# Eleven convolution taps moved into an attention's steps, selection rounds put between index sums, and waits for GpSimd's weight halves

## The chip, the cores and the metric

The kernel runs on one core of a Trainium2 chip. The metric is the device time of one execution in microseconds (us), lower is better. One execution was also recorded by the hardware profiler; its rows are what this document reads.

## The reference

Two transformer blocks on 512 tokens of width 1024, all in fp32. What bears on this change is the first block's mixer (windowed attention, a 31-tap depthwise convolution, memory attention) and the second block's sparse attention with its index scores and its top-128 choice:

```python
def conformer_conv(u, w_dw, b_dw, g_ln, b_ln):
    a, gate = jnp.split(u, 2, axis=-1)
    h = a * jax.nn.sigmoid(gate)
    h = lax.conv_general_dilated(h, w_dw[:, None, :], window_strides=(1,),
        padding=((CONV_WIDTH - 1, 0),), ...) + b_dw      # CONV_WIDTH = 31, 256 channels
    return jax.nn.silu(layer_norm(h, g_ln, b_ln))
...
    x = x + jnp.concatenate([y_attn, y_conv, y_mem], axis=-1) @ w_out[l]
...
    def block_fn(args):                                  # 4 blocks of 128 queries
        qb, qib, wib, start = args
        s = jnp.einsum('bqhd,bsd->bqhs', qib, ki)        # 8 index heads
        score = jnp.einsum('bqhs,bqh->bqs', jax.nn.relu(s), wib)
        score = jnp.where(causal[None], score, -jnp.inf)
        _, sel = lax.top_k(score, topk)                  # topk = 128
        ...                                              # attention over the chosen keys
```

## The kernel before, in words

Every engine has its own program, written out in order, and engines meet only at semaphores. Weights come in tiles of 128x1024 through a ring of four slots (`w_raw`). Each fp32 weight tile is split into a high half (`w_hi`, ScalarE, L1202) and a low half (`w_lo`: VectorE's `split`, L1561, in the feed-forward parts, GpSimd's `split`, L592, in two pieces of 512 columns, in the two attention mixers). A product is then three matmuls: high by high, low by high, high by low (L675 to L677). SyncE may load a ring slot again once the low half of its tile is done, and TensorE may use a tile once its low half is done.

The work runs in stages: feed-forward part, first mixer, feed-forward part, second mixer, and two more feed-forward parts with a convolution mixer between them. In a mixer, TensorE goes through the projection tiles (`TILES_A`, `TILES_B`) one by one; index m in the code counts the tile, and ScalarE and VectorE have the same loop over m for the tile one or more places behind. Inside tile m, after its third and sixth step of eight, TensorE does small things for earlier tiles (`betweenA`, `betweenB`): sums of squares of a head pair, the spread of its inverse norm (`head_spread`, L922, which needs the reciprocal of VectorE's `head_rstd`, L1786), or the scores of two index heads (`index_pair`, L1119).

After the tiles comes the attention: a loop over pairs of heads and query blocks, u = 0, 1, 2, ... In each step TensorE makes the scores of pair u (L951, mask L954), transposes the weights of pair u-2 (L972) and multiplies pair u-3 with the values (L993); VectorE takes the row maximum of pair u (`pair_max`, L1826 on), and in every second step normalises a group of two pairs (`group_norm`, L1863, on whose result the next group's values wait) and makes its low half (L1871); ScalarE takes the exponentials (L1363). What a step does besides is in `others(u)`. Scores of even pairs lie in PSUM banks 0 and 1, of odd pairs in banks 2 and 3.

The convolution of the first mixer is 62 VectorE instructions, taps t = 0 to 30 of channel half c = 0, then of c = 1 (`conv_tap`, L1928 and L1931), each adding one shifted, weighted copy of `glu` to an accumulator in bank 2 or 3; the last tap of a half writes `conv` in SBUF. `TAPS_AT` says how many taps stand at which m. All of them end before TensorE may score pair 1, whose banks they use. The mean over channels follows from `conv` by TensorE (`conv_total`, L1047, at u = 2) and VectorE (L1980, at u = 3).

In the second mixer, blocks b = 1, 2, 3 of 128 queries have (b+1)*128 scores each, summed over eight index heads (`index_sum`, L2015 and L2018, two heads after each `index_pair`). A selection round (`take_top`) takes the eight largest away: MAX8 (L2030), then MATCH_REPLACE8 (L2032). Each block takes 16 rounds, then a mask (L2035) on which the first score of that block's attention waits. `TOPS_AT` places rounds at m, and the rest goes one by one into the attention's steps u = 1, 2, ... (`topB`). A rope (`head_rope`) is three VectorE instructions on SBUF data, L1805, L1807 and L1809.

Of the kernel before, what the change touches and what calls it, by code (L numbers as in the profile page):

```python
# [23 lines left out]
TT = T // P  # L24
# [12 lines left out]
CONV_A = 31  # L37
# [47 lines left out]
def build(nc, A, out):  # L85
    ctx = ExitStack()
    with ctx:
# [72 lines left out]
        def chunk(t, k, width=T):  # L160
            return t[:, k * width:(k + 1) * width]
# [262 lines left out]
            TOPS += [(b, "tri")] + [(b, r, s) for r in range(ROUNDS) for s in ("max", "take")] + [(b, "mask")]  # L424
        top = Marks(sem("top"), TOPS)
        ROUND_LIST = [(b, r) for b in range(1, TT) for r in range(ROUNDS)]
        TOPS_AT = {9: 3, 10: 3, 11: 2, 12: 3, 13: 3, 14: 3, 15: 3, 16: 3, 17: 2}
        TOP_EARLY = sum(TOPS_AT.values())
        TAPS_AT = {2: 3, 3: 3, 4: 6, 5: 6, 6: 5, 7: 6, 8: 3, 9: 5, 10: 5, 11: 5, 12: 4, 13: 4, 14: 4, 15: 3}

        def index_slot(m, part):

# [35 lines left out]
        def after(eng, marks, key):  # L468

            eng.wait_ge(marks.sem, marks.value[key])  # L470
# [99 lines left out]
        def _(pool):  # L570
# [89 lines left out]
            pool.wait_ge(x_done, 32)  # L660
            pool.dma_start(matsB[:, :], A["mats"]).then_inc(stage_in, 16)
            for j in range(LEAD, len(TILES_B) + KC):
                split(first_job["mixB"] + j)
            after(pool, h_roped, "qB7")
            ada_steps(2)
# [3 lines left out]
        def _(pe):  # L669
# [371 lines left out]
            betweenA(len(TILES_A), 0)  # L1041

            def sumsA(u):
                if u == 2:
                    after(pe, d_conv, (CONV_A - 1, 1))
                    for c in range(2):
                        mm = pe.matmul(bank(5), ones[:, :], chunk(conv, c), start=c == 0, stop=c == 1)  # L1047
                    mm.then_inc(p_misc.at("conv_total"), 1)
                if 5 <= u < 5 + TT:
                    b = u - 5  # L1050
                    if b == 0:
                        after(pe, a_misc, "conv_sq1")
                    for c in range(2):
                        mm = pe.matmul(bank(5)[:, b:b + 1], hsA[:, c * T + b * P:c * T + (b + 1) * P], ones[:, 0:1],
                                       start=c == 0, stop=c == 1)
                    if b == TT - 1:
                        mm.then_inc(p_misc.at("conv_var"), 1)
                if u == len(PAIRS_A) + 2:
                    out_chunk("outA", 0, oA_hi, oA_lo, ("a", 1), True)
                    after(pe, d_misc, "conv_rstd")  # L1060
                    for b in range(TT):
                        mm = pe.matmul(bank(5)[:, b * P:(b + 1) * P],
                                       hrA[:, 64 + 32 + b:64 + 32 + b + 1].to_broadcast([P, P]), identity[:, :],
                                       start=True, stop=True)
                    mm.then_inc(p_misc.at("conv_spread"), 1)
                    for k in range(1, 4):
                        out_chunk("outA", k, oA_hi, oA_lo, ("a", 2 * k + 1))

            def scoreA(pair):
                kind, j, b = pair  # L1070
                if PAIRS_A.index(pair) == 1:
                    after(pe, d_conv, (CONV_A - 1, 1))
                if b == 0 and kind == "win":
                    after(pe, h_roped, f"qA{j}")
                if b == 0 and kind == "mem":
                    after(pe, h_normed, f"mk{j}")
                    after(pe, h_scaled, f"mq{j}")
                    after(pe, v_done, f"mv{j}")
                if kind == "win":
                    n, lo = (P, 0) if b == 0 else (2 * P, (b - 1) * P)  # L1080
                    pair_score(pair, lambda rows: qA[rows, j * T + b * P:j * T + (b + 1) * P],
                               lambda rows: kA[rows, lo:lo + n], ident16A[:, :], mask16A[:, 2 * P - n:2 * P])
                else:
                    pair_score(pair, lambda rows: mq[rows, j * T + b * P:j * T + (b + 1) * P],
                               lambda rows: mk[rows, j * M:(j + 1) * M], None, None)
# [110 lines left out]
        def _(act):  # L1196
# [224 lines left out]
            for m in range(2, len(TILES_A) + 1):  # L1421
                t = TILES_A[m - 1]
# [36 lines left out]

            def conv_part(u):  # L1460

                if u == 4:
                    for c in range(2):
                        after(act, d_misc, f"ctr{c}")
                        act.activation(chunk(hsA, c), chunk(conv, c), ACT.Square).then_inc(a_misc.at(f"conv_sq{c}"), 1)
                if u == 25:
                    after(act, p_misc, "conv_var")
                    act.activation(hrA[:, 32:32 + TT], bank(5)[:, 0:TT], ACT.Sqrt, bias=tiny[:, 0:1], scale=1.0 / (2 * P))\
                        .then_inc(a_misc.at("conv_std"), 1)
                if u == 26:  # L1470
                    for c in range(2):
                        after(act, d_misc, f"conv_n{c}")
                        act.activation(chunk(conv, c), chunk(conv, c), ACT.Silu, bias=col("cln_b", c))\
                            .then_inc(a_misc.at(f"conv_y{c}"), 1)
                if u == 27:
                    for c in range(2):
                        after(act, a_misc, f"conv_y{c}")
                        act.activation(oA_hi[4 + c], chunk(conv, c), ACT.Copy).then_inc(g_hi.at(f"c{c}"), 1)
# [77 lines left out]
        def _(dve):  # L1556
# [366 lines left out]
            def conv_tap(t, c):  # L1923
                src = glu[:, c * (PAD_A + T) + t:c * (PAD_A + T) + t + T]
                w = col("w_dw", c * CONV_A + t)
                if t == 0:
                    after(dve, glu_done, f"a{c}")
                    dve.tensor_scalar(bank(2 + c), src, w, col("b_dw", c), ALU.mult, ALU.add).then_inc(d_conv.at((t, c)), 1)  # L1928
                else:
                    after(dve, d_conv, (t - 1, c))  # L1930
                    dve.scalar_tensor_tensor(chunk(conv, c) if t == CONV_A - 1 else bank(2 + c), src, w, bank(2 + c),  # L1931
                                             ALU.mult, ALU.add).then_inc(d_conv.at((t, c)), 1)

            done = 0
# [39 lines left out]
                    query_inverse("A", 8 * len(QUERIES[0]), qscA, qnsA)  # L1974

            def conv_part(u):
                if u == 3:
                    after(dve, p_misc, "conv_total")
                    for c in range(2):
                        dve.scalar_tensor_tensor(chunk(conv, c), bank(5), -1.0 / (2 * P), chunk(conv, c), ALU.mult,  # L1980
                                                 ALU.add).then_inc(d_misc.at(f"ctr{c}"), 1)
# [59 lines left out]
            for m in range(2, len(TILES_B) + 1):  # L2041
# [11 lines left out]
                              chunk({"kB": kB, "qB": qB, "qi": qi}[r[:2]], int(r[2])))  # L2053
                if m == 4:
                    head_rstd("ki")
                for b, r in ROUND_LIST[done:done + TOPS_AT.get(m, 0)]:
                    take_top(b, r)
                done += TOPS_AT.get(m, 0)
                for b, h in index_step(m):
                    index_sum(b, h)  # L2060
                if n in h_normed.value and m > 3:
                    head_norm(n, straight(n))

# [169 lines left out]
```

## Time and profile before

| what | value |
|---|---|
| median of 3 runs | 2165.54 us (2160.98 to 2165.81) |
| the profiled execution's own time | 2165.37 us |
| its span, first to last instruction | 2163.4 us |
| TensorE busy | 2135.3 us, 99% |
| VectorE busy | 1211.7 us, 56% |
| ScalarE busy | 783.2 us, 36% |
| GpSimd busy | 233.8 us, 11% |
| granted TensorE clock, mean | 0.994 |

TensorE is busy nearly all the time, so the kernel gets shorter only where TensorE waits, or where it runs at its lower clock. In the profile PE is TensorE, DVE VectorE, ACT ScalarE, POOL GpSimd.

### The profile page before, as it was taken

What the parts mean: (1) busy time and instruction counts of PE and PEld (TensorE: products, weight loads), DVE (VectorE), ACT (ScalarE), POOL (GpSimd) and SP (SyncE); (2) the same over time, 40 slices, a digit from 0 to 9 for tenths busy, and PEclk for the clock granted to TensorE, in tenths of its full rate; (3) what the DMA queues carried; (4) which work ended last, traced back from release to release, by engine and by line L of the source; (5) the groups of instructions that cost most, each with busy time, mean ns of one, the idle gap of its engine ahead of it and who ended that gap; (6) DMA issues with size and microseconds to landing.
All of it is one profiled execution on the core that took longest, in us unless ns stands there. A gap on an engine that the chain in (4) does not pass through costs nothing.

```text
span 2163.4 us, 28943 instructions
## 1 busy us (share of the span) xinstructions
PE 2135.3 (99%) x10238; PEld 1758.0 (81%) x10238; DVE 1211.7 (56%) x1760; ACT 783.2 (36%) x1081; POOL 233.8 (11%) x237
## 2 busy tenths in 40 slices
PE   9999999999999999999989999999999999999999
PEld 8888888877888888877767888888888878888887
DVE  7555444886566554465796575554456456333333
ACT  6222333547442223334355342223333234222222
POOL 0000201650200030014300200000000000000000
PEclk9999999999999999999989999999999999999999
DMA  5555333320345542323300245542332222222232
GB/s 190 183 185 184 104 95 109 124 82 2 107 156 184 187 136 83 93 93 113 107 21 1 85 139 185 185 155 74 101 117 90 95 88 89 96 97 97 78 99 85
DMA packets 75733, 242.96 MB, mean 112 GB/s; under 512 B 9328, under 2 KB 9584, under 8 KB 75536
## 3 DMA queue, kind: packets, MB, share of 16 engines
q1 hardware_dynamic: 61376, 189.61, 26.9%
q0 software_dynamic: 14288, 52.44, 7.8%
q8 instruction: 43, 0.70, 0.1%
q14 instruction: 26, 0.21, 0.0%
HBM read 235.65 MB, written 2.10 MB: 110 GB/s over the span
## 4 chain that ended last, share of the span: by engine, by line
PE 89%; DVE 8%; ACT 1%; issue 1%; DMA 0%; SPq 0%; ACTq 0%; DVEq 0%
PE ps L675 27%; PE ps L677 27%; PE ps L676 27%; PE ps L993 2%; DVE ps L1931 2%; PE ps L951 1%; PE ps L972 1%; PE ps L770 1%; DVE tmp L1604 1%; DVE score L2032 1%; DVE top L2030 1%; PE ps L954 1%; PE ps L1119 0%; DVE w_lo L1561 0%; DVE ropB L1805 0%
## 5 line engine op out<-in xcount | busy, mean ns | idle before, releaser
L675 PE MATMUL ps<-h_hi,w_hi 128*128 128x512 f32 x1888 | 743.3, 394 | 1.3 <-DVE h_lo L1871 0.9
L677 PE MATMUL ps<-h_hi,w_lo 128*128 128x512 f32 x1888 | 735.8, 390 | 0.0
L676 PE MATMUL ps<-h_lo,w_hi 128*128 128x512 f32 x1888 | 735.3, 389 | 0.0
L1561 DVE TENSOR_TENSOR w_lo<-w_raw,w_hi 128x1024 fp32r<-128x1024 f32 x336 | 412.8, 1230 | 433.3 <-ACT w_hi L1202 418.3
L1202 ACT ACTIVATE w_hi<-w_raw 128x1024 fp32r<-128x1024 f32 x383 | 402.3, 1051 | 247.0 <-PE ps L677 245.5
L675 PEld LDWEIGHTS ps<-h_hi,w_hi 128*128 128x128 f32 x1888 | 354.0, 187 | 81.0 <-issue 7.1
L677 PEld LDWEIGHTS ps<-h_hi,w_lo 128*128 128x128 f32 x1888 | 353.8, 187 | 76.2
L676 PEld LDWEIGHTS ps<-h_lo,w_hi 128*128 128x128 f32 x1888 | 354.1, 188 | 72.7 <-issue 0.2
L675 PE MATMUL ps<-hid_hi,w_hi 128*128 128x512 f32 x704 | 273.9, 389 | 0.0
L676 PE MATMUL ps<-hid_lo,w_hi 128*128 128x512 f32 x704 | 273.9, 389 | 0.0
L677 PE MATMUL ps<-hid_hi,w_lo 128*128 128x512 f32 x704 | 273.9, 389 | 0.0
L1274 ACT ACTIVATE hid_hi<-tmp 128x512 f32 (+1 forms) x88 | 55.6, 632 | 394.7 <-DVE tmp L1716 385.9
L592 POOL TENSOR_TENSOR w_lo<-w_raw,w_hi 128x512 fp32r<-128x512 f32 x100 | 134.7, 1368 | 573.0 <-ACT w_hi L1202 571.6
L675 PEld LDWEIGHTS ps<-hid_hi,w_hi 128*128 128x128 f32 x704 | 132.1, 188 | 27.5
L677 PEld LDWEIGHTS ps<-hid_hi,w_lo 128*128 128x128 f32 x704 | 132.1, 188 | 27.5
L676 PEld LDWEIGHTS ps<-hid_lo,w_hi 128*128 128x128 f32 x704 | 132.1, 188 | 27.3
L1271 ACT ACTIVATE tmp<-ps 128x512 f32<-128x512 f32 x83 | 49.6, 598 | 245.4 <-PE ps L677 245.3
L1716 DVE TENSOR_TENSOR tmp<-tmp,ps 128x512 f32<-128x512 f32 x83 | 57.1, 687 | 142.5 <-PE ps L677 142.5
L1670 DVE SCALAR_TENSOR_TENSOR ada_sum<-ada_raw,c_act,ada_sum 128x512 f32<-128x512 f32 x168 | 125.8, 749 | 3.4
L576 POOL DMA_DIRECT2D ada_raw<-in_ada_w x96 | 51.5, 537 | 598.1 <-DVE ada_sum L1670 577.7
L1676 DVE TENSOR_TENSOR hid_lo<-tmp,hid_hi 128x512 f32 (+1 forms) x88 | 61.2, 695 | 77.9 <-ACT hid_hi L1274 77.9
L1212 ACT ACTIVATE tmp<-x 128x512 f32 (+1 forms) x56 | 35.3, 630 | 160.3 <-DVE x L1583 159.9
(304 smaller groups left out, 1749.1 us busy)
## 6 DMA issues: line engine op xcount, KB each, us to landing
ada_raw<-in_ada_w POOLq DMA_DIRECT2D x96, 512.0 KB, 4.3
w_raw<-in_gate SPq DMA_DIRECT2D x88, 512.0 KB, 3.5
w_raw<-in_up SPq DMA_DIRECT2D x88, 512.0 KB, 3.5
w_raw<-in_down SPq DMA_DIRECT2D x64, 384.0 KB, 3.0
w_raw<-in_down SPq DMA_DIRECT2D x64, 320.0 KB, 2.8
w_raw<-in_w_mix_c SPq DMA_DIRECT2D x24, 512.0 KB, 3.5
w_raw<-in_w_mix_b SPq DMA_DIRECT2D x17, 512.0 KB, 3.5
w_raw<-in_w_mix SPq DMA_DIRECT2D x16, 512.0 KB, 3.5
```

Source lines behind the costliest of these rows:

```text
L576: pool.dma_start(ada_raw[:, (piece % 2) * 2 * ADA:(piece % 2 + 1) * 2 * ADA], src.rearrange("a p n -> (a p) n")).then_inc(ada_in[piece % 2 ...
L592: low = pool.tensor_tensor(w_lo[:, at:at + WT // 2], w_raw[:, at:at + WT // 2], f32(w_hi[:, at:at + WT // 2]), ALU.subtract)
L675: pe.matmul(dest, s_hi, m_hi, start=first and n == 0, stop=False)
L676: pe.matmul(dest, s_hi, m_lo, start=False, stop=False)
L677: mm = pe.matmul(dest, s_lo, m_hi, start=False, stop=last and n == len(pairs) - 1)
L1202: act.activation(chunk(w_hi, slot, WT), chunk(w_raw, slot, WT), ACT.Copy).then_inc(w_hi_done, 1)
L1271: act.activation(chunk(tmp, u), bank(s), ACT.Silu).then_inc(silu_done, 1)
L1274: act.activation(hid_hi[:, bass.ds(i * (2 * T) + u * T, T)], chunk(tmp, 2 + u), ACT.Copy)\
L1561: dve.tensor_tensor(chunk(w_lo, slot, WT), chunk(w_raw, slot, WT), f32(chunk(w_hi, slot, WT)), ALU.subtract).then_inc(w_lo_done, 1)
L1670: dve.scalar_tensor_tensor(ada_sum[:, :], w, c_act[:, k:k + 1], ada_sum[:, :], ALU.mult, ALU.add).then_inc(ada_sum_done, 1)
L1676: dve.tensor_tensor(hid_lo[:, at], chunk(tmp, 2 + u), f32(hid_hi[:, at]), ALU.subtract)\
L1716: dve.tensor_tensor(chunk(tmp, 2 + u), chunk(tmp, u), bank(s), ALU.mult)\
```

## The change

Three things are changed. The last 11 of the 62 taps leave m = 13 to 15 (and m = 12 keeps its four) and go one by one into the steps u = 1 to 11 of the first attention; they add in SBUF (`conv`) and no longer in bank 3, and the mean's steps move from u = 2, 3, 4 to u = 13, 14, 15, its variance from u = 5 on to u = 16 on. In the second mixer nine more selection rounds stand ahead of the attention (34 of 48 for 25), some between the two pairs of index sums of one m. And GpSimd's low half of tile 9 waits for the rope of qi3, those of tiles 10 and 11 for the index sums (1, 5) and (2, 1), and those of tiles 15 to 20 for the ropes of qB0 to qB5.

```diff
-        TOPS_AT = {9: 3, 10: 3, 11: 2, 12: 3, 13: 3, 14: 3, 15: 3, 16: 3, 17: 2}
+        TOPS_AT = {8: (0, 1), 9: (4, 1), 10: (5, 2), 11: (4, 1), 12: (0, 2), 13: (3, 0), 14: (3, 0), 15: (3, 0), 16: (3, 0),
+                   17: (2, 0)}
...
-        TAPS_AT = {2: 3, 3: 3, 4: 6, 5: 6, 6: 5, 7: 6, 8: 3, 9: 5, 10: 5, 11: 5, 12: 4, 13: 4, 14: 4, 15: 3}
+        TAPS_AT = {2: 3, 3: 3, 4: 6, 5: 6, 6: 5, 7: 6, 8: 3, 9: 5, 10: 5, 11: 5, 12: 4}
+        LATE_TAPS = 2 * CONV_A - sum(TAPS_AT.values())
+        LEAVES_BANK = [CONV_A - 1, CONV_A - LATE_TAPS - 1]
...
             for j in range(LEAD, len(TILES_B) + KC):
+                if j == 9:
+                    after(pool, h_roped, "qi3")
+                if j == 10:
+                    after(pool, i_sum, (1, 5))
+                if j == 11:
+                    after(pool, i_sum, (2, 1))
+                if 15 <= j <= 20:
+                    after(pool, h_roped, f"qB{j - 15}")
                 split(first_job["mixB"] + j)
...
             def sumsA(u):
-                if u == 2:
+                if u == LATE_TAPS + 2:
                     after(pe, d_conv, (CONV_A - 1, 1))
...
                 if PAIRS_A.index(pair) == 1:
-                    after(pe, d_conv, (CONV_A - 1, 1))
+                    after(pe, d_conv, (LEAVES_BANK[1], 1))
...
-                    dve.scalar_tensor_tensor(chunk(conv, c) if t == CONV_A - 1 else bank(2 + c), src, w, bank(2 + c),
+                    dve.scalar_tensor_tensor(chunk(conv, c) if t >= LEAVES_BANK[c] else bank(2 + c), src, w,
+                                             chunk(conv, c) if t > LEAVES_BANK[c] else bank(2 + c),
                                              ALU.mult, ALU.add).then_inc(d_conv.at((t, c)), 1)
...
             def conv_part(u):
-                if u == 3:
+                if 1 <= u <= LATE_TAPS:
+                    conv_tap(CONV_A - LATE_TAPS - 1 + u, 1)
+                if u == LATE_TAPS + 3:
                     after(dve, p_misc, "conv_total")
...
-                for b, r in ROUND_LIST[done:done + TOPS_AT.get(m, 0)]:
-                    take_top(b, r)
-                done += TOPS_AT.get(m, 0)
-                for b, h in index_step(m):
-                    index_sum(b, h)
+                for part in range(2):
+                    rounds = TOPS_AT.get(m, (0, 0))[part]
+                    for b, r in ROUND_LIST[done:done + rounds]:
+                        take_top(b, r)
+                    done += rounds
+                    for b, h in index_slot(m, part):
+                        index_sum(b, h)
```

In the changed file the lines stand 3 to 14 further down: L1786 is L1797, L1931 is L1942, L1826 is L1837, L2018 is L2032.

VectorE's program at the end of the first mixer's tiles, before: eight taps (m = 12 and 13), the reciprocal for the first memory key tile, four taps, its norm, the query inverses, the second reciprocal, three taps.

```order
212 L1931 SCALAR_TENSOR_TENSOR ps<-glu,cols,ps 128x512 x8
213 L1786 RECIPROCAL hrA<-hrA 128x4
214 L1931 SCALAR_TENSOR_TENSOR ps<-glu,cols,ps 128x512 x4
215 L1799 TENSOR_TENSOR mk<-mk,ps 128x256
216 L1813 RECIPROCAL qinv<-qstd 128x48
219 L1786 RECIPROCAL hrA<-hrA 128x4
220 L1931 SCALAR_TENSOR_TENSOR ps<-glu,cols,ps 128x512 x2
221 L1931 SCALAR_TENSOR_TENSOR conv<-glu,cols,ps 128x512
```

The same place of the changed kernel:

```order
212 L1942 SCALAR_TENSOR_TENSOR ps<-glu,cols,ps 128x512 x3
213 L1942 SCALAR_TENSOR_TENSOR conv<-glu,cols,ps 128x512
214 L1797 RECIPROCAL hrA<-hrA 128x4
215 L1810 TENSOR_TENSOR mk<-mk,ps 128x256
216 L1824 RECIPROCAL qinv<-qstd 128x48
219 L1797 RECIPROCAL hrA<-hrA 128x4
220 L1810 TENSOR_TENSOR mk<-mk,ps 128x256
```

Four taps stand ahead of the first reciprocal where eight stood, and none behind it.

VectorE's program in steps u = 3 and 4 of the first attention of the changed kernel (before, the same rows stood there without the L1942 rows, and with two of L1980 at u = 3):

```order
240 L1837 TENSOR_REDUCE small<-ps 128x2
241 L1845 TENSOR_TENSOR small<-small,qnsA 128x2
242 L1847 SCALAR_TENSOR_TENSOR small<-sink,small 128x2
243 L1849 TENSOR_TENSOR small<-sink,small 128x2
244 L1866 TENSOR_TENSOR small<-small,ps 128x4
245 L1869 RECIPROCAL small<-small 128x4
246 L1874 TENSOR_TENSOR osbA<-ps,small 128x256
247 L1942 SCALAR_TENSOR_TENSOR conv<-glu,cols,conv 128x512
248 L1837 TENSOR_REDUCE small<-ps 128x2
```

One tap stands behind each step's maximum and group work, ahead of the next step's maximum.

VectorE's program at m = 9 and 10 of the second mixer, before:

```order
565 L2018 SCALAR_TENSOR_TENSOR score<-relu,wi,score 128x384 x4
566 L1786 RECIPROCAL hrB<-hrB 128x8
567 L2030 MAX top<-score 128x8
568 L2032 MATCH_REPLACE score<-top,score 128x256
...
573 L2018 SCALAR_TENSOR_TENSOR score<-relu,wi,score 128x384 x2
574 L2015 TENSOR_SCALAR score<-relu,wi 128x512
```

And of the changed kernel:

```order
578 L2032 SCALAR_TENSOR_TENSOR score<-relu,wi,score 128x384 x2
579 L2044 MAX top<-score 128x8
580 L2046 MATCH_REPLACE score<-top,score 128x256
581 L2032 SCALAR_TENSOR_TENSOR score<-relu,wi,score 128x384 x2
582 L1797 RECIPROCAL hrB<-hrB 128x8
...
593 L2032 SCALAR_TENSOR_TENSOR score<-relu,wi,score 128x384 x2
594 L2044 MAX top<-score 128x8
595 L2046 MATCH_REPLACE score<-top,score 128x256
```

The index sums that ran on end have rounds between them; rows 583 to 592, left out, are five rounds where three stood.

## Rows read from the trace of the kernel before

**Rows 1.** Stretches: us, busy us by engine (instructions), clock, DMA share, GB/s

```profile
470.00:481.00 11.00, 10.53 (x65) 9.47 (x65) 6.07 (x13) 3.23 (x7) 2.51 (x2) 0.70 0.23 83
481.00:508.00 27.00, 26.69 (x212) 20.86 (x208) 17.55 (x64) 18.46 (x44) 0.00 (x0) 1.00 0.00 1
1005.00:1046.00 41.00, 41.00 (x210) 28.59 (x211) 22.14 (x49) 18.23 (x35) 11.83 (x10) 1.00 0.24 78
1046.00:1091.00 45.00, 44.16 (x228) 36.95 (x227) 43.37 (x85) 16.90 (x25) 16.25 (x12) 0.96 0.41 118
1091.00:1114.60 23.60, 17.33 (x130) 13.00 (x129) 22.53 (x68) 12.82 (x34) 0.00 (x0) 0.93 0.01 1
1114.60:1125.00 10.40, 10.38 (x48) 8.53 (x48) 8.53 (x22) 5.21 (x11) 0.00 (x0) 0.52 0.01 2
```

**Rows 2.** Waits of TensorE, whole span: us in total, times, longest

```profile
PE ps L922 <- DVE hrA L1786: 4.1, 1, 4.1
PE ps L993 <- DVE osbB L1863: 3.5, 3, 2.4
PE ps L951 <- ACT pB L1363: 2.6, 3, 1.2
...
PE ps L951 <- DVE dmask L2035: 1.9, 1, 1.9
...
PE ps L1119 <- DVE ki L1809: 1.2, 1, 1.2
```

**Rows 3.** Timeline of TensorE, end of the first mixer's tiles

```profile
464.82 0.28 PE L677 MATMUL ps<-mh_hi,w_lo 128*128 128x256 f32 x1
469.21 0.66 PE L922 MATMUL ps<-identity,hrA 128*64 128x128 f32 x8 [4.11 <-DVE hrA L1786]
...
480.00 0.49 PE L951 MATMUL ps<-kA,qA 64*128 64x128 f32 x4
```

**Rows 4.** Timeline of VectorE, same place: start, us, line, what, count

```profile
462.79 6.29 DVE L1931 SCALAR_TENSOR_TENSOR ps<-glu,cols,ps 128x512 f32<-128x512 f32 x8
468.99 0.17 DVE L1786 RECIPROCAL hrA<-hrA 128x4 f32<-128x4 f32 x1
469.11 3.13 DVE L1931 SCALAR_TENSOR_TENSOR ps<-glu,cols,ps 128x512 f32<-128x512 f32 x4
```

**Rows 5.** Waits of VectorE from 481.7 to 508.4, steps u = 1 to 11

```profile
DVE small L1826 <- PE ps L954: 7.8, 7, 2.3
```

**Rows 6.** Timeline, steps u = 2 and 3 of the first attention

```profile
485.28 0.69 DVE L1826 TENSOR_REDUCE small<-ps 128x2 f32<-128x512 f32 x1 [2.27 <-PE ps L954]
...
489.37 1.28 DVE L1980 SCALAR_TENSOR_TENSOR conv<-ps,conv 128x512 f32<-128x512 f32 x2
```

**Rows 7.** Timeline of TensorE, step u = 2: the channel mean's sum

```profile
485.30 1.88 PE L1047 MATMUL ps<-conv,ones 128*128 128x512 f32 x4
```

**Rows 8.** Line L1809, 985 to 1090: ns min/median/max, first and last start

```profile
L1809 DVE TENSOR_TENSOR qi<-ropB x4: 691/692/1640, 987.9 to 1004.0; 128x512 f32<-128x512 f32 x4
```

**Rows 9.** Timeline of VectorE, index sums of block 3, second mixer

```profile
1044.59 1.61 DVE L2018 SCALAR_TENSOR_TENSOR score<-relu,wi,score 128x512 f32<-128x512 f32 x2 [1.73 <-ACT relu L1525]
...
1055.44 3.35 DVE L2018 SCALAR_TENSOR_TENSOR score<-relu,wi,score 128x512 f32<-128x512 f32 x2
```

**Rows 10.** Timeline of GpSimd, second mixer: low half of tile 16

```profile
1055.26 2.98 POOL L592 TENSOR_TENSOR w_lo<-w_raw,w_hi 128x512 fp32r<-128x512 f32 x2 [4.44 <-ACT w_hi L1202]
```

**Rows 11.** Selection rounds by shape, 1000 to 1160: busy us, mean ns

```profile
L2030 DVE MAX8 top<-score 128x8 f32<-128x512 f32 x16 | 11.0, 686 | 0.0
L2030 DVE MAX8 top<-score 128x8 f32<-128x384 f32 x16 | 8.9, 556 | 0.2
...
L2030 DVE MAX8 top<-score 128x8 f32<-128x256 f32 x16 | 6.7, 420 | 0.4
```

**Rows 12.** Timeline, start of the second attention on TensorE and on VectorE

```profile
1086.40 0.49 PE L951 MATMUL ps<-kB,qB 64*128 64x128 f32 x4
...
1091.44 0.42 DVE L1826 TENSOR_REDUCE small<-ps 128x2 f32<-128x256 f32 x1
```

More of the change, by code:

```diff
@@ L426, in build @@
         ROUND_LIST = [(b, r) for b in range(1, TT) for r in range(ROUNDS)]
-        TOPS_AT = {9: 3, 10: 3, 11: 2, 12: 3, 13: 3, 14: 3, 15: 3, 16: 3, 17: 2}
-        TOP_EARLY = sum(TOPS_AT.values())
-        TAPS_AT = {2: 3, 3: 3, 4: 6, 5: 6, 6: 5, 7: 6, 8: 3, 9: 5, 10: 5, 11: 5, 12: 4, 13: 4, 14: 4, 15: 3}
+        TOPS_AT = {8: (0, 1), 9: (4, 1), 10: (5, 2), 11: (4, 1), 12: (0, 2), 13: (3, 0), 14: (3, 0), 15: (3, 0), 16: (3, 0),
+                   17: (2, 0)}
+        TOP_EARLY = sum(before + between for before, between in TOPS_AT.values())
+        TAPS_AT = {2: 3, 3: 3, 4: 6, 5: 6, 6: 5, 7: 6, 8: 3, 9: 5, 10: 5, 11: 5, 12: 4}
+        LATE_TAPS = 2 * CONV_A - sum(TAPS_AT.values())
+        LEAVES_BANK = [CONV_A - 1, CONV_A - LATE_TAPS - 1]
         def index_slot(m, part):
@@ L1048, in sumsA @@
                     mm.then_inc(p_misc.at("conv_total"), 1)
-                if 5 <= u < 5 + TT:
-                    b = u - 5
+                if LATE_TAPS + 5 <= u < LATE_TAPS + 5 + TT:
+                    b = u - LATE_TAPS - 5
                     if b == 0:
@@ L1460, in conv_part @@
             def conv_part(u):
-                if u == 4:
+                if u == LATE_TAPS + 4:
                     for c in range(2):
```

## The prediction

> **What bounds the kernel now.** I read the page first: TensorE is 99% busy, so only its waits and its low-clock stretches can be won. The list of TensorE's waits [rows 2] puts the longest at the end of the first mixer's tiles (4.1 us, for the reciprocal of L1786) and the next in the second attention: 3.5 us for VectorE's group norms, 2.6 for exponentials, 1.9 for the mask of block 3; and 1.2 us ahead of it for the rope of ki. The table of stretches [rows 1] adds the clock: 0.70 of full speed in 470 to 481, right behind the 4.1 us wait, and 0.52 in 1114.6 to 1125, behind several short ones. In it TensorE is the bound in steps u = 1 to 11 of the first attention (26.7 of 27 us busy, VectorE 17.6), and VectorE is the bound from 1046 to 1114.6 (43.4 of 45 and 22.5 of 23.6 us). From 1005 to 1046 VectorE is busy 22.1 of 41 us. So the second mixer has a slack stretch and behind it a full one, and the first attention has slack on VectorE.
>
> My sum is made against the profiled execution: span 2163.4 us, 2.0 us around it, 2165.4 us, 0.2 below the median shown.
>
> **First mixer, end of the tiles.** TensorE ends its products at 464.82 + 0.28 = 465.1 and waits until 469.21 [rows 3] for a reciprocal that starts at 468.99, behind eight taps of 6.29 us from 462.79 on: 0.79 each [rows 4]. With four taps ahead of it, it starts 4 x 0.79 = 3.1 us earlier, at 465.9, and TensorE's wait shrinks from 4.1 to 1.0: **-3.1**. Late next is then the same reciprocal, by that 1.0. The seven taps behind it (3.13 us for four of them) go too, so that the second reciprocal is no later than TensorE wants it. The clock was 0.70 over the next 11 us: 0.30 x 11 = 3.3 us lost. The wait of 1.2 us for ki [rows 2] is near in size, and the stretch from 1005 on that follows it has a clock of 1.00 [rows 1], so behind a wait of 1.0 I expect no dip: **-3.3**. Bounds: 0 if it falls all the same, -3.3 if not. GpSimd's and ScalarE's tile work there is on time now and follows TensorE.
>
> **First attention.** Eleven taps of 0.79 are 8.7 us on VectorE; the row of such a pass that reads SBUF twice is 0.80, two in 1.61 us [rows 9]. VectorE's waits for scores in these steps are 7.8 us [rows 5], and the two passes of L1980, 1.28 us [rows 6], leave for u = 14. Of the first wait, 2.27 us ahead of u = 2 [rows 6], only one tap (0.8) fits, so usable are 7.8 - 1.5 + 1.3 = 7.6 of the 8.7: VectorE is 1.1 us late at u = 12. Besides, TensorE's sum L1047 (1.88 us [rows 7]) moves from u = 2, ahead of these steps, to u = 13, behind them. In the stretch VectorE now sets the pace, so its leaving buys nothing, and where it lands TensorE is the bound: +1.9. Together **+3.0**. Bounds: 0, since the same work as a sum fits the waits to within 0.4 us (8.7 against 7.8 + 1.3), and 8.7, all taps on the path. I take 3.0, nearer the fit, as each wait is used up where it stands. The taps' order is a chain, but each is ready long before its turn; TensorE's score of pair 1 needs only the tap that ends in m = 12.
>
> First mixer in all: -3.1 - 3.3 + 3.0 = -3.4.
>
> **Second mixer.** *Tile 9's low half* ran under the rope of ki. A rope's L1809 takes 0.69 us alone and 1.64 beside GpSimd [rows 8]. Behind qi3 the ki rope is some 1.9 us shorter (two such instructions), more than TensorE's wait of 1.2: **-1.2**. What is queued behind GpSimd's waits: its next low halves (3.0 us each [rows 10]), SyncE's loads of the tiles four further on and the rope transfers behind those. TensorE wants tile j three tiles after its ring slot came free, and GpSimd is idle 4.4 us ahead of such a half [rows 10]; a delay of about one tile, some 6 us, fits in. If not, TensorE stops at that tile.
>
> *The rounds.* One round is two passes of equal length [rows 11]: about 0.9, 1.2 and 1.4 us for 256, 384 and 512 scores. Ahead of 1046 there were 8, now 18. Ten more, at most 10 x 1.2 = 12 us, stand against 41 - 22.1 = 18.9 us of slack: **0**, as long as no index sum is late by more than the half tile between two of TensorE's index pairs. Without that cover each would cost its 0.9.
>
> *The full stretch 1046 to 1091* had 17 rounds, 8 short and 9 middle: 18.0 us, and two small steps around block 2; it now has 14 middle and 2 long: 19.6 us, with the same two small steps for blocks 2 and 3. +1.6 against a mask step and a mask sum that no longer meets GpSimd, 1.4: about 0. What is saved is contention: three rope instructions run beside a low half there, each up to 0.95 longer [rows 8], say 0.85, and a pair of sums takes 3.35 for 1.61 [rows 9] beside the low half of 1055.26 [rows 10]: 2.55 + 1.75 = 4.3. But the wait for qB0 releases tile 15's half exactly when the sums (3, 6) and (3, 7) start, so I give 1.75 back: **-2.5** (bounds 0 and -4.3). The Trainium skill (SBUF - State Buffer, "Who interferes with whom") says that a VectorE instruction with two SBUF inputs and a GpSimd one that reads SBUF exclude each other, and whoever starts first goes through; the trace agrees, with 1.64 for 0.69 [rows 8]. By it the first sum could win and the saving be nearer 4.3; and max and replace, with one SBUF input, would cost nothing beside GpSimd, which is where the waits put it.
>
> VectorE reaches the second attention at 1091.44, TensorE at 1086.40 [rows 12]: 5 us of lateness that TensorE covers with idle matmuls and waits. From 1091 to 1114.6 it idles 23.6 - 17.3 = 6.3 us [rows 1]. There VectorE has in u = 1 to 7 long rounds for middle ones, 7 x 0.2 = 1.4, less 0.7 for the mask steps done before: **+0.7**. Of the 1.2 + 2.5 - 0.7 = 3.0 us, TensorE makes 1.2 itself and finds 1.8 of its 6.3 in waits.
>
> *Block 3's mask* is ready at u = 14 and not at u = 23; TensorE's wait of 1.9 before u = 24 goes: **-1.9**. The nine rounds leave steps where TensorE was the bound, which gives nothing.
>
> Second mixer: -1.2 - 2.5 + 0.7 - 1.9 = -4.9. Sum: -3.4 - 4.9 = -8.3, so **2165.4 - 8.3 = 2157.1**.
>
> **The rivals.** A difference under 0.3% (6.5 us) is about what a measurement of this kernel can't tell from none.
>
> *The clock takes a part back* (20%). Either it falls behind the 1.0 us wait all the same (+3.3), or once in the first attention. There VectorE has no slack in u = 4 to 11, so TensorE stops briefly in each second step, as it did in 1091 to 1114.6, and then 0.48 x 10.4 = 5.0 us were lost [rows 1]. Against it: about 3 us of stops in 27, there 6.3 in 23.6. Result 2157.1 + 3.3 = 2160.4 to 2157.1 + 5.0 = 2162.1. The Trainium skill (TensorE: Matmul & The Clock Gate, "A second HAM failure mode: psum-queue depth-cycling") has short stops between groups of matmuls swing the clock between its two levels; the trace shows such a swing in the second attention, 0.52, and none in the first, 1.00 [rows 1].
>
> *The second attention's low stretch goes* (15%). Its stops are fewer, and 1114.6 to 1125 may run at full clock. VectorE still has its rounds there, so I count 3.5 of the 5.0 us: 2153.6.
>
> *The second mixer gives little* (13%): contention only moves to the sums and TensorE's waits stay, since VectorE's full stretch is as long as before. Then -3.4 - 1.2 = -4.6: 2160.8.
>
> *Slower* (6%): the first attention is held to the pace of VectorE and TensorE falls to the low clock again and again, 5.0 us each time. From three such stretches on it is slower: -8.3 + 15.0 = +6.7, 2172.1. For it: u = 4 to 11 is paced by VectorE. Against it: once the clock is low TensorE is the slower engine and stops hardly any more (10.38 of 10.4 us busy), and the low stretch ended after 10.4 us [rows 1].
>
> **How the numbers follow.** The forecast has 46%, with a range of its own of 2154.5 to 2159.7 (the taps' 3.0 down to 1.0, the contention's 2.5 from 0 to 4.3). 80% over all cases: 2151.5 to 2162.5, which leaves out half of the slower case and the ends of the others. Faster by over 0.3%, below 2159.0 by the median: four fifths of the forecast (37), all of the third rival (15), a tenth or two of the others (4): 0.56. Slower 0.05. The same: 0.39.
>
> **What would show it.** The wait of TensorE for the reciprocal (now L1797) at about 1 us and the clock at 1.00 behind it; first pair score some 6.4 us earlier against the product before it; VectorE's waits in u = 2 to 11 gone but for one or two; no wait for ki, none for the mask of block 3; ropes qB0 to qB5 at 0.69 an instruction, the sums (3, 6) and (3, 7) at 3.3; VectorE at the second attention's first maximum 3 to 4 us nearer to TensorE. The prediction is wrong if the first attention grows by over 5 us, if TensorE waits for a low half, or if the clock dips at new places.

## The result: 0.4% slower

The changed kernel takes 2173.84 us (median of 5 executions, 2168.32 to 2174.68), the kernel before beside it 2165.54 us (5 executions, 2160.98 to 2166.33). The ratio is 1.0039, with a 95% interval of 1.0023 to 1.0056: slower, where 2157.1 us was forecast. The profiled execution of the changed kernel is its fastest one, 2168.32 us with a span of 2166.5 us and a mean granted clock of 0.990; the other four have 0.987. The profile therefore shows 3 us of the loss at most, and some 5 us of it happened in executions that left no trace.

TensorE's waits in the changed kernel (total in us, times, longest), to be held against [rows 2]. The line numbers of TensorE's program are 11 higher there than in the kernel before:

```profile
PE ps L1004 <- DVE osbB L1874: 3.6, 4, 2.6
PE ps L686 <- DVE y_lo L2134: 2.3, 1, 2.3
PE ps L1065 <- ACT hsA L1476: 2.0, 1, 2.0
PE ps L962 <- ACT pB L1374: 1.3, 2, 0.7
...
PE ps L933 <- DVE hrA L1797: 0.9, 1, 0.9
```

Read it by what is missing and by what is new. The wait of 4.1 us for the reciprocal is 0.9 now, those for the rope of ki (1.2) and for block 3's mask (1.9) are gone. All three went as forecast. One line is new: 2.0 us of TensorE's variance sums (L1065, before L1054) for ScalarE's squares.

By the waits alone the kernel should be faster. The table of stretches says why it isn't (columns as in [rows 1], the granted clock stands behind POOL):

```profile
466.00:481.00 15.00, 14.27 (x117) 11.50 (x117) 6.93 (x21) 7.38 (x17) 4.71 (x4) 1.00 0.30 107
481.00:508.00 27.00, 26.28 (x200) 19.74 (x202) 22.76 (x76) 17.93 (x46) 0.00 (x0) 1.00 0.00 1
508.00:541.00 33.00, 30.93 (x161) 25.19 (x159) 13.64 (x40) 15.66 (x34) 0.00 (x0) 0.64 0.00 1
...
1005.00:1046.00 41.00, 41.00 (x217) 29.16 (x215) 31.87 (x77) 18.51 (x35) 14.60 (x12) 1.00 0.31 100
1046.00:1091.00 45.00, 45.00 (x221) 36.10 (x220) 43.01 (x88) 16.00 (x24) 16.48 (x13) 1.00 0.40 119
...
1105.00:1115.00 10.00, 8.62 (x42) 6.71 (x43) 9.49 (x27) 4.70 (x13) 0.00 (x0) 0.51 0.00 1
```

Behind the first mixer the clock is 1.00 now. But from 508 to 541 us it is 0.64, and 0.36 x 33 = 11.9 us of full-speed work are lost. In the kernel before the same stretch ran at 1.00:

```profile
508.00:541.00 33.00, 31.79 (x251) 25.78 (x249) 19.05 (x62) 24.88 (x54) 0.00 (x0) 1.00 0.01 2
```

TensorE's timeline of the changed kernel shows where the low level begins:

```profile
507.77 0.70 PE L962 MATMUL ps<-kA,qA 64*128 64x256 f32 x4
...
510.91 1.00 PE L1004 MATMUL ps<-vA,pTA 128*128 128x65 f32 x8
513.87 0.61 PE L1065 MATMUL ps<-ones,hsA 128*128 128x1 f32 x4 [1.96 <-ACT hsA L1476]
514.41 0.90 PE L962 MATMUL ps<-mk,mq 64*128 64x256 f32 x4
...
516.14 1.81 PE L1004 MATMUL ps<-vA,pTA 128*128 128x65 f32 x8
...
518.95 1.22 PE L962 MATMUL ps<-mk,mq 64*128 64x256 f32 x4
```

The same instructions take 1.00 us ahead of the stop of 1.96 us and 1.81 behind it: 2.4 GHz before, 1.2 GHz after. The low level lasts to about 539 us, though TensorE is never idle in it (24.00 us busy from 515 to 539).

Where TensorE stands against the kernel before, from its timeline: the first pair score comes 6.4 us earlier (473.64 for 480.00), the spread of the convolution's norm behind the first attention 7.9 us later (548.07 for 540.2), the first index pair 6.6 us later, the end of the second mixer still 6.6 later, and the first product behind the second attention 1.6 us later (1209.36 for 1207.73). Behind it two short dips of the clock, which cost about 1.7 us each (1250 to 1255 us runs at 0.71, 1745 to 1760 at 0.89), stand against one such dip in the kernel before (1800 to 1810 us at 0.83) and bring the 1.6 us to the 3.1 us of the span. So up to the first pair score 6.4 us were won, in the first attention 14.2 lost, and in the second mixer and the second attention 6.3 won.

### The profile page after: what moved, and what is told of

It is laid out like the page before. It is cut to its first block, busy times and chain, and to the rows that moved or that the text cites. A ratio compares the mean times of both kernels' runs of the same rounds, so it can differ in the third digit from the quotient of the medians.

```text
span 2166.5 us, 28943 instructions
## 1 busy us (share of the span) xinstructions
PE 2143.9 (99%) x10238; PEld 1763.8 (81%) x10238; DVE 1206.1 (56%) x1760; ACT 782.6 (36%) x1081; POOL 236.0 (11%) x237
## 4 chain that ended last, share of the span: by engine, by line
PE 91%; DVE 7%; ACT 1%; issue 1%; ACTq 0%; DVEq 0%
PE ps L686 28%; PE ps L688 27%; PE ps L687 27%; PE ps L1004 2%; DVE ps L1942 1%; PE ps L962 1%; PE ps L983 1%; DVE tmp L1615 1%; PE ps L781 1%; PE ps L713 1%; DVE small L1837 1%; PE ps L965 0%; PE ps L1130 0%; DVE ropA L1818 0%; DVE w_lo L1572 0%
```

## The experiments

Twelve kernels ran, each beside the kernel before on the same chip. The ratios are those on record with their intervals, and not quotients of the medians (for e5 the medians would give 1.0090).

| run | median us (range, executions) | ratio to before (95%) |
|---|---|---|
| e1, taps only | 2176.8 (2161.0 to 2185.6, 10) | 1.0047 (1.0021 to 1.0074) |
| e2, second mixer only | 2159.1 (2158.2 to 2165.1, 10) | 0.9983 (0.9974 to 0.9993) |
| e3, variance later | 2157.5 (2154.0 to 2179.6, 10) | 0.9982 (0.9962 to 1.0002) |
| e4, filler | 2158.0 (2156.2 to 2163.3, 10) | 0.9972 (0.9959 to 0.9984) |
| e5, sums late, taps not | 2184.6 (2172.4 to 2197.3, 5) | 1.0070 (1.0036 to 1.0104) |
| e6, two fillers | 2155.4 (2153.9 to 2156.0, 5) | 0.9949 (0.9932 to 0.9967) |
| e7, GpSimd's waits only | 2161.8 (2158.8 to 2170.3, 10) | 0.9986 (0.9973 to 1.0000) |
| e8, rounds only | 2162.2 (2159.0 to 2170.7, 10) | 0.9986 (0.9973 to 0.9999) |
| e9, short fillers | 2155.9 (2151.9 to 2157.3, 6) | 0.9949 (0.9931 to 0.9968) |
| e10, one step earlier | 2154.5 (2152.8 to 2159.6, 7) | 0.9954 (0.9938 to 0.9970) |
| e11, earlier and filler | 2154.9 (2150.7 to 2155.1, 5) | 0.9944 (0.9923 to 0.9965) |
| e12, wait put back | 2169.9 (2157.0 to 2179.0, 10) | 1.0009 (0.9984 to 1.0033) |

The kernel before had medians of 2163.97 us beside e1 to e4 (31 executions), 2165.04 beside e5 to e8 (21) and 2163.71 beside e9 to e12 (19).

### Which part loses: e1 and e2

e1 is the kernel before with the part of the diff on the convolution alone, e2 the changed kernel with that part undone.

```diff
 # e1, against the kernel before (and the steps of total, centring, squares and sums as in the change)
-        TAPS_AT = {2: 3, 3: 3, 4: 6, 5: 6, 6: 5, 7: 6, 8: 3, 9: 5, 10: 5, 11: 5, 12: 4, 13: 4, 14: 4, 15: 3}
+        TAPS_AT = {2: 3, 3: 3, 4: 6, 5: 6, 6: 5, 7: 6, 8: 3, 9: 5, 10: 5, 11: 5, 12: 4}
 # e2, against the changed kernel: the same two lines the other way round, so that LATE_TAPS is 0
```

> The kernel before with the convolution part alone: eleven taps late, and total, centring, squares and variance sums moved with them; rounds and GpSimd as before. Theory (the loss is made in the first attention, where TensorE waits 1.96 us for the squares and then runs at the low clock): the first attention's end stands 7.9 us later than before, so 2165.4 + 7.9 = 2173 us, with the 2.0 us wait and a stretch of about 25 us near a granted clock of 0.5 behind it. Rival (the second mixer's part costs, and the first attention's loss is a matter of one execution): within 3 us of before or some 3 us below it.

> The changed kernel with the convolution part undone: all taps in the first mixer, total, centring, squares and sums as before; the rounds and GpSimd's waits as changed. Theory: in the changed kernel TensorE gained 1.2 us at the rope of ki and 5.0 us in the second attention, so 2165.4 - 6.2 = 2159 us, TensorE without a wait for ki or for block 3's mask. Rival (the second mixer's part is what costs): 2168 us or more.

Both came out as the theory has them: e1 alone is slower than before (2176.8 us for 2173), and e2 gains 4.8 us (2159.1 for 2159). e1 shows the same stop (2.0 us for the squares) and a clock of 0.63 from 508 to 541. Its executions lie 25 us apart, from 2161.0 to 2185.6. The loss is in the convolution's part, and its size changes from one execution to the next.

### Taps or steps: e5

```diff
 # kernel before, all taps in their places; LATE = 11
-                if u == 2:
+                if u == LATE + 2:          # total (TensorE)
...
-                if 5 <= u < 5 + TT:
+                if LATE + 5 <= u < LATE + 5 + TT:   # variance sums
...
-                if u == 4:
+                if u == LATE + 4:          # squares (ScalarE)
...
-                if u == 3:
+                if u == LATE + 3:          # centring (VectorE)
```

> The kernel before with all its taps where they were; only the total, the centring, the squares and the variance sums of the convolution stand eleven steps later, as in the changed kernel. Theory 1 (the steps that were moved along with the taps make the wait, through the centring that delays a maximum and the squares that follow its exponential): TensorE waits about 2 us for the squares at u = 16 and mostly falls to the low clock; the first mixer's 4.1 us wait stays; 2164 + 2 + some 10, 2173 to 2180 us. Theory 2 (eleven taps on VectorE make it late): no such wait, 2164 us within 3.

2184.6 us, above the 2173 to 2180 expected, with the same stop of 1.96 us although VectorE has no late tap at all:

```profile
518.10 0.61 PE L1057 MATMUL ps<-ones,hsA 128*128 128x1 f32 x4 [1.96 <-ACT hsA L1468]
...
515.00:555.00 40.00, 37.30 (x178) 32.10 (x176) 12.32 (x37) 17.65 (x38) 0.00 (x0) 0.56 0.00 1
```

The stop needs no late tap: the four steps that had to move with the taps make it. (That late taps without it do no harm is shown by e10 below.) Their chain in the changed kernel, from the timeline of VectorE and ScalarE:

```profile
506.82 0.69 DVE L1837 TENSOR_REDUCE small<-ps 128x2 f32<-128x512 f32 x1 [2.65 <-PE ps L965]
...
509.10 1.28 DVE L1994 SCALAR_TENSOR_TENSOR conv<-ps,conv 128x512 f32<-128x512 f32 x2
...
510.29 0.68 DVE L1837 TENSOR_REDUCE small<-ps 128x2 f32<-128x512 f32 x1
...
511.40 1.02 ACT L1374 ACTIVATE pA<-ps,small,qscA 128x256 f32<-128x256 f32 x2 [1.53 <-DVE small L1847]
...
512.67 1.15 ACT L1476 ACTIVATE hsA<-conv 128x512 f32<-128x512 f32 x2
```

The total (L1058, 1.88 us) stands on TensorE ahead of the score that VectorE wants next, so VectorE idles 2.65 us and then centres at 509.10. The centring holds up the maximum of step 15, ScalarE's exponentials wait for it until 511.40, and the squares stand behind these: they end at 513.8 (512.67 + 1.15). TensorE came to its variance sums at 511.91.

### The stop or the work: e4, e3 and e12

e4 puts matmuls of ones into the gap, and nothing comes earlier by it. e3 leaves out the stop at that place by moving the sums two steps on.

```diff
 # e4
                     if b == 0:
+                        after(pe, d_misc, "ctr1")
+                        for _ in range(16):
+                            pe.matmul(bank(5)[:, 0:P], ones[:, :], ones[:, :], start=True, stop=True)
                         after(pe, a_misc, "conv_sq1")
 # e3
-                if LATE_TAPS + 5 <= u < LATE_TAPS + 5 + TT:
-                    b = u - LATE_TAPS - 5
+                if LATE_TAPS + 7 <= u < LATE_TAPS + 7 + TT:
+                    b = u - LATE_TAPS - 7
```

> The changed kernel with sixteen extra matmuls of ones (2.0 us by the 2.47 us of twenty such ones of L713) ahead of TensorE's wait for the squares, into a part of the bank that the variance sums overwrite: the wait is filled, nothing comes earlier. Theory 1 (it is TensorE's idleness that drops the clock): granted clock 1.00 through the first attention, 11.9 us below the changed kernel, so 2168.3 - 11.9 = 2156 to 2162 us (against its profiled run and its median). Theory 2 (the wait is no cause; the late taps' load or the memory pairs' steps make the low clock): the same time as the changed kernel, 2168 to 2174 us, low clock again.

> The changed kernel with one edit: TensorE's variance sums of the convolution stand two steps later (u = 18 to 21 for 16 to 19). Theory 1 (TensorE's wait for the squares drops the clock): no wait for the squares; ScalarE's copy of the weights of step 16 still comes behind the squares, which leaves up to 1.1 us of wait at u = 17, about that of the end of the first mixer, behind which the clock stayed at 1.00; 0.9 us and the 11.9 us of low clock come back, 2156 us. Theory 2 (the steps of the memory pairs run at the low clock behind any stop, the 1.1 us too): 2167 to 2173 us, low clock again from step 17 on.

e4 takes 2158.0 us, 6.0 us below the kernel before on its chip, where the changed kernel was 8.3 above: 14 us, for work that is of no use to anybody:

```profile
511.84 3.79 PE L1065 MATMUL ps<-ones 128*128 128x128 f32 x32
515.47 0.50 PE L1068 MATMUL ps<-ones,hsA 128*128 128x1 f32 x4
...
508.00:541.00 33.00, 32.02 (x254) 27.43 (x255) 16.98 (x50) 21.83 (x45) 0.00 (x0) 1.00 0.01 1
```

The clock stays at 1.00 from 508 to 541. (The filler was larger than meant: each matmul of ones is two records of 0.12 us, so the sixteen took 3.79 us in place of 1.96, and the sums end 1.5 us later than without them. In e9 below half the number, 2.00 us, holds the clock there as well.) All ten executions lie within 7.1 us.

e3 is a mixed answer. Its median is about what theory 1 said, but two of its ten executions took 2174.0 and 2179.6 us. The profiled one is the slowest, and it shows two shorter stops with the low level behind them:

```profile
513.32 0.70 PE L962 MATMUL ps<-mk,mq 64*128 64x256 f32 x4 [0.55 <-ACT pA L1374]
515.21 0.65 PE L983 MATMUL ps<-matsA,pA 128*128 128x128 f32 x4 [1.19 <-ACT pTA L1382]
...
516.00:557.00 41.00, 40.25 (x176) 35.05 (x176) 10.04 (x30) 16.44 (x32) 0.00 (x0) 0.50 0.00 1
```

So a stop of 1.2 us with one of 0.55 ahead of it can do it too. By their mean granted clock, 0.984 and 0.986 for 0.992 to 0.996, it did so in two of the ten executions.

e12 is the converse. It is e10 below, whose longest stop in the first attention is 0.75 us, and gets a longer one by a single wait, at which nothing is computed:

```diff
                 # e10's places of the four steps, and at the end of step 16:
+                if u == 16:
+                    after(pe, u_exp, PAIRS_A[16] + (1,))
```

> The steps one earlier, and one wait put in: at the end of step 16 TensorE waits for the exponentials of its own step's scores, which takes about 2 us as the wait for the squares did. Nothing else differs, and no computation waits longer for it than for TensorE itself. Theory (a stop of 2 us there is enough for the low clock): TensorE at the low clock behind it in most executions, as in the changed kernel: 2154 + 2 + some 8 to 12, 2163 to 2170 us. Rival (the stop must meet the squares, the centring or the late taps): 2154 + 2 = 2156 us.

```profile
514.59 0.80 PE L962 MATMUL ps<-mk,mq 64*128 64x256 f32 x4 [1.26 <-ACT pA L1376]
515.32 1.11 PE L983 MATMUL ps<-matsA,pA 128*128 128x128 f32 x4
...
515.00:558.00 43.00, 42.25 (x185) 36.01 (x182) 12.31 (x33) 17.51 (x33) 0.00 (x0) 0.52 0.00 1
```

The stop is 1.26 us long, less than meant. It costs 15.4 us of median against e10 on the same chip. Four of the ten executions stayed at 2157 to 2162.4, six lie between 2168 and 2179. The profiled one is nearly all of 43 us at the low level: 0.48 x 43 = 20.6 us lost, with TensorE busy for 42.25 of them.

### The steps in a better place: e10

The four steps stand one step earlier each, all eleven taps are still late.

```diff
-                if u == LATE_TAPS + 2:     # total, now + 1
-                if u == LATE_TAPS + 3:     # centring, now + 2
-                if u == LATE_TAPS + 4:     # squares, now + 3
-                if LATE_TAPS + 5 <= u < LATE_TAPS + 5 + TT:   # variance, now + 4
```

> The changed kernel with the convolution's total, centring, squares and variance sums one step earlier each (u = 12, 13, 14, 15 to 18 for 13, 14, 15, 16 to 19), all eleven taps still late, no filler. Theory (the place of these steps makes the wait): VectorE sat idle for 2.65 us ahead of the maximum of step 14 and now centres there, ScalarE squares in an even step, TensorE does not wait; no low clock in the first attention. Against the kernel with the first filler, 2158.0 less its 3.8 us: 2154 us. Rival (the late taps themselves, or the memory pairs' steps, bring TensorE to the low clock): 2165 us or more.

```profile
510.12 0.61 PE L1065 MATMUL ps<-ones,hsA 128*128 128x1 f32 x4 [0.47 <-ACT hsA L1476]
...
508.00:541.00 33.00, 31.55 (x237) 26.29 (x234) 15.97 (x46) 22.59 (x46) 0.00 (x0) 1.00 0.01 1
```

2154.5 us, 9.2 below the kernel before on that chip, where the changed kernel was 8.3 above it on its own. The stop is 0.47 us and the clock 1.00. From the first pair score to the spread of the convolution's norm it takes 61.8 us (473.78 to 535.6), for 60.2 in the kernel before and 74.4 in the changed one.

### The second mixer's part: e7 and e8

e7 has GpSimd's nine waits alone, e8 the new places of the rounds alone.

```diff
 # e7, against the kernel before
+                if j == 9:
+                    after(pool, h_roped, "qi3")
...
+                if 15 <= j <= 20:
+                    after(pool, h_roped, f"qB{j - 15}")
 # e8, against the kernel before (with the loop over the two halves of a step)
-        TOPS_AT = {9: 3, 10: 3, 11: 2, 12: 3, 13: 3, 14: 3, 15: 3, 16: 3, 17: 2}
+        TOPS_AT = {8: (0, 1), 9: (4, 1), 10: (5, 2), 11: (4, 1), 12: (0, 2), 13: (3, 0), 14: (3, 0), 15: (3, 0), 16: (3, 0),
+                   17: (2, 0)}
```

> The kernel before with GpSimd's nine waits alone; rounds and taps as before. By the prediction's terms: the wait for ki goes (1.2 us) and VectorE gets 2.5 us less contention ahead of the second attention, of which TensorE keeps about 1.5: 2164.0 - 2.7 = 2161 us, block 3's mask wait of 1.9 us still there. Rival (contention only moves onto the index sums): 1.2 us alone, 2163 us.

> The kernel before with the new places of the selection rounds alone; GpSimd and taps as before. By the prediction's terms: block 3's mask wait of 1.9 us goes, the wait for ki stays, VectorE enters the second attention about as late as before (5.0 us behind TensorE): 2164.0 - 1.9 + 0.7 = 2163 us. Rival (more rounds ahead of the full stretch are what brings VectorE nearer to TensorE): VectorE's first maximum under 3 us behind TensorE's first score, 2160 us or less.

The first maximum of VectorE and the first score of TensorE in the second attention, of e7 and then of e8 (5.04 us apart in the kernel before, [rows 12]):

```profile
1086.06 0.49 PE L961 MATMUL ps<-kB,qB 64*128 64x128 f32 x4
1087.43 0.42 DVE L1836 TENSOR_REDUCE small<-ps 128x2 f32<-128x256 f32 x1
```

```profile
1085.58 0.49 PE L954 MATMUL ps<-kB,qB 64*128 64x128 f32 x4
1090.48 0.42 DVE L1829 TENSOR_REDUCE small<-ps 128x2 f32<-128x256 f32 x1
```

GpSimd's waits bring VectorE 3.7 us nearer (1.37 us late), the rounds hardly anything (4.90). e7 has no wait for ki, but still 1.9 us for the mask; e8 the other way round. Both gain 2.9 to 3.2 us of median, together 6.1, more than the 4.8 of e2; with intervals of some 3 us to either side that is no contradiction and no proof of a sum.

### Fillers in the second attention: e6, e9 and e11

e6 adds twenty matmuls of ones to e4 at u = 5 of the second attention, ahead of TensorE's wait of 2.63 us for VectorE's group norm. e9 has both fillers at half the number. e11 is e10 with ten such matmuls there.

```diff
                 if X % 2 == 0 and G >= 1:
+                    if X == len(PAIRS_A) + 2:
+                        idle(20)           # e9 and e11: idle(10)
                     after(pe, o_norm, GROUPS[G - 1])
```

> The kernel with sixteen filling matmuls in the first attention, and twenty more (2.5 us) in the second attention's wait of 2.63 us for VectorE's group norm at u = 5. Theory (idleness drops the clock here too): the stretch of 8.3 us at the low clock that follows that wait (1096.1 to 1104.4) goes, but VectorE has its rounds there, so between 1.5 and 4.2 us below the kernel with one filler: 2154 to 2156.5 us. Rival (the clock falls in the second attention from several small stops, or VectorE holds the pace anyway): the same as with one filler, 2158 us.

> The kernel with both fillers, at half their length: the trace showed each filling matmul twice at 0.12 us, so that sixteen took 3.79 us where 1.96 were idle. Now eight at the wait for the squares (1.9 us) and ten at u = 5 of the second attention (2.4 us). Theory: the clock stays at 1.00 and the surplus of 1.8 us in the first attention is saved, and up to 2 us in the second (where VectorE holds the pace, so I count 0.5): 2155.4 - 2.3 = 2153 us. Rival (the surplus was what kept the clock up): low stretches are back, 2158 us or more.

> The steps one earlier as in the run beside it, and ten filling matmuls (2.4 us) in the second attention's wait for VectorE's group norm at u = 5. Theory: both low stretches gone without surplus work: 2.6 us below the one without the filler, 2151 to 2152 us. Rival (without a filler in the first attention the low clock comes back there in some executions): a spread of over 8 us between the executions.

The stretch from 1091 to 1125 in e6, and the same in e9:

```profile
1091.00:1125.00 34.00, 30.23 (x244) 23.62 (x242) 32.86 (x86) 18.37 (x45) 0.00 (x0) 1.00 0.01 2
```

```profile
1091.00:1125.00 34.00, 29.86 (x221) 22.55 (x221) 32.83 (x86) 18.72 (x45) 0.00 (x0) 0.95 0.01 2
```

e6 did what was expected: 2155.4 for 2158.0, and the low stretch is gone (e4 ran at 0.50 from 1095 to 1100 us and at 0.55 from 1100 to 1105). e9 and e11 missed: 2155.9 for the expected 2153, and 2154.9 for 2151 to 2152. In the first attention e9's filler of 2.00 us, just as long as the stop, holds the clock:

```profile
508.00:541.00 33.00, 31.90 (x244) 26.86 (x244) 17.32 (x50) 22.95 (x46) 0.00 (x0) 1.00 0.01 1
```

In the second attention its filler of 2.40 us leaves 0.30 us of the wait of 2.63, and the clock stays up behind it. It falls 5 us later, behind two further stops:

```profile
1098.36 0.49 PE L962 MATMUL ps<-kB,qB 64*128 64x128 f32 x4 [0.71 <-ACT pB L1379]
...
1099.99 0.63 PE L1006 MATMUL ps<-vB,pTB 128*128 128x65 f32 x4 [0.70 <-DVE osbB L1879]
...
1100.77 0.90 PE L962 MATMUL ps<-kB,qB 64*128 64x256 f32 x4
```

In e6, with 4.63 us of filler, TensorE does not stop at these two places. That the longer filler gave VectorE the time to catch up, and that e9 and e11 (0.95 too) lose by the dip what they save on filler, is likely and was not tried. The fillers in the second attention are no gain over e10 that these runs can tell.

## Why the prediction was wrong

**The step that failed** is the first attention, "Together +3.0". It counted the taps, the total (L1047) and the centring (L1980), and it left out, without a reason, the two steps behind them, the squares and the variance sums, which move by the same eleven steps. They cost TensorE a stop of 1.96 us, and this stop cost the clock: the first attention grew by 14.2 us in the profiled execution, not by 3.0. Two of the prediction's own signs of being wrong came true by it: the first attention grew by over 5 us, and the clock dipped at a new place. That the moved steps do it and not the taps is shown by e5 and e10; that the stop does it and not the squares' work, by e4 (the gap filled, the clock held) and by e12 (a stop alone, 15.4 us). The remaining median of the changed kernel, 5 us above its profiled execution at a clock lower by 0.003 (0.003 x 2172 = 6.5 us), fits a longer low stretch as in e3, e5 and e12. That was not seen in a trace of the changed kernel itself.

**The rivals.** The rival that ends slower had the right place and the right agent, TensorE's low clock in the first attention, with 6%. Its mechanism and its price were wrong, and that its 2172.1 us lies within 2 us of the 2173.8 measured is luck. It wanted three stretches from VectorE's pace that lose 5.0 us each; one stretch behind a single stop lost 11.9 us in the profiled execution of the changed kernel, and 20.6 in that of e12. Nearer was a half of the 20% rival, that the clock falls once in the first attention, but it too had VectorE's pace for the cause and 5.0 us for the price. The argument against the slower rival, "the low stretch ended after 10.4 us", took the length of the one case at hand for a rule. The Trainium skill (TensorE: Matmul & The Clock Gate, "A second HAM failure mode: psum-queue depth-cycling") says that frequent short stops between groups of matmuls swing the clock; here one stop decided, since filling it alone kept the clock at 1.00 (e4).

**The first mixer's end, -3.1 and -3.3:** right. The wait is 0.94 us, the clock 1.00 behind it, the first score 6.36 us earlier for 6.4 forecast. The inference behind it, that a stop of about 1 us does no harm, held here in every profile with the late taps (466 to 481 us at 1.00 in e1, e3, e4, e10 and e12), but a stop of 1.2 or 1.26 us in the first attention was not harmless, and neither was one of 0.77 us in the norm at 1249 us of the changed kernel (0.71 behind it, where the kernel before has the same stop and 1.00). It was a fact of its place and of the execution, not a rule.

**The taps on VectorE and L1047:** about right. With the steps in a better place (e10) the first attention grows by 1.6 us for the 3.0 counted, within its bounds of 0 to 8.7.

**The second mixer, -4.9:** right. 6.3 us came in the profiled execution, 4.8 of median in e2. The wait for ki went (-1.2) and that for block 3's mask too (-1.9). VectorE comes to the second attention 1.9 us behind TensorE (1094.88 for 1093.02) where it was 5.0 [rows 12]: 3.2 us nearer, for 3 to 4 forecast. GpSimd's waits alone bring it 3.7 us nearer (e7), more than the 2.5 taken. The rope instructions of qB take 0.69 us each, as forecast. The sums (3, 6) and (3, 7) take 2.44 us together, not the 3.3 that was given back to GpSimd:

```profile
1056.78 0.69 DVE L1820 TENSOR_TENSOR qB<-ropB 128x512 f32<-128x512 f32 x1
1057.39 2.44 DVE L2032 SCALAR_TENSOR_TENSOR score<-relu,wi,score 128x512 f32<-128x512 f32 x2
...
1057.55 3.43 POOL L595 TENSOR_TENSOR w_lo<-w_raw,w_hi 128x512 fp32r<-128x512 f32 x2 [10.71 <-DVE qB L1820]
```

The first sum began 0.16 us ahead of GpSimd's half, and only one of the two sums is long (1.59 us). The Trainium skill (SBUF — State Buffer, "Who interferes with whom") says that whoever starts first goes through; the trace agrees, with GpSimd's pair at 3.43 us for 2.5 undisturbed.

**The second attention's low stretch** stayed (1105 to 1115 us at 0.51), as the forecast had it.

The sum of the other terms was sound. e10, which is the changed kernel with the four steps one earlier each, is 9.2 us below the kernel before; the forecast was 8.3. Its parts are off both ways: the first attention costs 1.6 us for 3.0, and the second mixer brings more than 4.9 in the profiled execution of the changed kernel.

## What to carry to other kernels

When a step is moved, list everything that must move with it, down to the last consumer, and look for the engine that will stand in front of each one at its new place. The cheap link of the chain (0.6 us of sums here) is the one that stops the engine that sets the time. In this kernel a stop of TensorE of 1.2 to 2 us in the first attention cost itself, and in some or most executions twelve to twenty us by the low clock behind it: judge such a stop by several executions, since the one in the profile may be the lucky one, and before rebuilding an order try a few matmuls of ones in the gap, which cost two lines and show at once whether the clock is what is lost.

## What was not expected of the hardware

- A short stop is followed by a long stretch at 1.2 GHz, with TensorE busy nearly all the time (but for one wait of 0.75 us in e3, e5 and e12): behind 1.96 us some 24 us (changed kernel, 0.64 over 33 us) and some 37 us (e5), behind 1.26 us some 41 us (e12, 0.52 over 43), behind 0.55 and 1.19 us 41 us (e3, 0.50 over 41). In the kernel before, the stretch behind the 4.1 us wait had a clock of 0.70 over 11 us, and the one in the second attention ended after 10.4 [rows 1]. In the changed kernel the level rose at about 539 us, still within the memory pairs; in e3, e5 and e12 only at 556 to 557 us, when the products of 512 columns behind the attention had begun (at 552.41, 555.76 and 551.62). Why it lasts so much longer in the steps of the memory pairs was not tried and stays open.
- Whether the clock falls behind such a stop changes between executions of one kernel: in e12 six of ten took 2168 us or more at a mean granted clock of 0.984 to 0.989, and four stayed below 2163 at 0.993 to 0.995; in e3 two of ten took 2174 us or more. In the executions without a profile only the mean says so, not the place.
- Matmuls of ones hold the clock when they are just as long as the gap: 2.00 us for a stop of 1.96 in the first attention (e9, 1.00 from 508 to 541 us). In the second attention 4.63 us for a gap of 2.63 held it (e6, 1.00 from 1091 to 1125 us), and 2.40 us left 0.95 (e9), by a dip that stands behind two later stops of 0.7 us.
